# Issuing a mixture's output weights from ScalarE's DMA queue

## What is computed

```python
def moe(h, router_w, router_b, w1, w3, w2):
    ...                       # the router gives every token two of 16 experts: comb
    y = jnp.zeros_like(h)
    for e in range(N_EXPERTS):
        y = y + comb[:, e:e + 1] * ((jax.nn.silu(h @ w1[e]) * (h @ w3[e])) @ w2[e])
    return y
```

## Time and profile before

| | us |
|---|---|
| median of three runs | 1736.25 |
| lowest, highest | 1732.82, 1738.97 |
| the profiled execution, its own time | 1744.38 |
| its span in the trace | 1742.8 |
| PE busy | 1582.3 (91%) |
| ACT busy | 342.9 (20%) |
| SyncE's queue (q1): bytes, share of the 16 DMA engines | 322.90 MB, 52.0% |
| ScalarE's queue (q10) | 10.31 MB, 1.7% |

### The profile page before, as it was taken

One profiled execution on the slowest core, in us unless ns is written; L12 is line 12 of the kernel. 1 busy time (PEld: TensorE's weight loads), 2 busy tenths in 40 slices (PEclk: granted clock), 3 DMA queues, 4 the chain that ended last, 5 costly groups with the idle time before them and its releaser, 6 DMA issues.

```text
span 1742.8 us, 27293 instructions
## 1 busy us (share of the span) xinstructions
PE 1582.3 (91%) x11510; PEld 1119.3 (64%) x11510; DVE 592.6 (34%) x1457; ACT 342.9 (20%) x760; POOL 81.6 (5%) x131
## 2 busy tenths in 40 slices
PE   6999999999889999999796799999849998899987
PEld 5787678876634856745443699998736575455544
DVE  2514422334245247105715111111055543233223
ACT  1313211122131123025204000000042223000000
POOL 0010000100110000000100200000010001000000
PEclk9899898999989899988898899999959998899999
DMA  8366353656765321120730699999783113999996
GB/s 257 94 202 194 124 158 92 197 169 207 199 193 167 101 95 50 49 73 1 229 135 29 256 386 401 394 402 392 314 292 118 73 49 108 338 391 388 391 402 270
DMA packets 180762, 365.11 MB, mean 210 GB/s; under 512 B 18868, under 2 KB 137488, under 8 KB 164160
## 3 DMA queue, kind: packets, MB, share of 16 engines
q1 hardware_dynamic: 164640, 322.90, 52.0%
q0 software_dynamic: 9984, 30.63, 5.5%
q10 hardware_dynamic: 6048, 10.31, 1.7%
HBM read 343.42 MB, written 20.40 MB: 209 GB/s over the span
## 4 chain that ended last, share of the span: by engine, by line
PE 77%; DMA 8%; DVE 8%; ACT 3%; issue 2%; POOL 1%; SPq 0%; POOLq 0%; ACTq 0%; DVEq 0%
PE ps_proj L622 30%; PE ps_outp L622 13%; PE ps_proj L1192 7%; PE ps_outp L1192 7%; PE ps_score L1192 7%; DMA ring<-in_exp_w 4%; PE ps_score L622 2%; PE ps_turn L775 2%; PE ps_outp L1294 2%; PE ps_proj L748 2%; DMA h_t<-in_exp_w 1%; PE ps_score L793 1%; DVE probs L2085 1%; DMA arena<-expert_in 1%; DMA ring<-in_w_in 1%
## 5 line engine op out<-in xcount | busy, mean ns | idle before, releaser
L622 PE MATMUL ps_proj<-h_t,ring 128*128 128x256 f32 (+1 forms) x1280 | 363.1, 444 | 13.6 <-ACT h_t L1733 8.1
L622 PEld LDWEIGHTS ps_proj<-h_t,ring 128*128 128x128 f32 x1280 | 252.3, 199 | 119.9 <-issue 84.9
L1192 PE MATMUL ps_proj<-ring,arena 128*32 128x128 f32 (+2 forms) x1824 | 127.3, 390 | 4.7 <-ACT arena L1882 2.5
L1192 PE MATMUL ps_outp<-ring,arena 128*32 128x384 f32 (+3 forms) x1600 | 123.4, 415 | 3.9 <-DVE arena L2455 3.2
L1192 PE MATMUL ps_score<-ring,arena 128*32 128x384 f32 (+2 forms) x1824 | 123.1, 381 | 4.1 <-DMA ring<-in_exp_w 4.1
L1192 PEld LDWEIGHTS ps_proj<-ring,arena 128*32 128x32 f32 (+1 forms) x1824 | 110.1, 117 | 22.2 <-issue 12.7
L1192 PEld LDWEIGHTS ps_score<-ring,arena 128*32 128x32 f32 (+1 forms) x1824 | 102.9, 114 | 24.5 <-issue 13.3
L1192 PEld LDWEIGHTS ps_outp<-ring,arena 128*32 128x32 f32 (+1 forms) x1600 | 88.3, 115 | 31.1 <-DVE arena L2455 5.6
L622 PE MATMUL ps_proj<-ring,h_t 128*128 128x256 f32 (+1 forms) x512 | 107.6, 368 | 0.4 <-ACT arena L1759 0.4
L622 PEld LDWEIGHTS ps_proj<-ring,h_t 128*128 128x128 f32 x512 | 93.9, 195 | 14.9 <-issue 3.6
L1579 ACT ACTIVATE arena<-ps_proj 128x512 f32<-128x512 f32 (+1 forms) x68 | 39.0, 576 | 324.1 <-PE ps_proj L622 323.2
(11 more groups left out here) (327 smaller groups left out, 1764.6 us busy)
## 6 DMA issues: line engine op xcount, KB each, us to landing
ring<-in_exp_w SPq DMA_DIRECT2D x152, 1024.0 KB, 11.3
ring<-in_ada_w SPq DMA_DIRECT2D x48, 1024.0 KB, 5.4
ring<-in_w_in SPq DMA_DIRECT2D x30, 1024.0 KB, 6.1
arena<-in_exp_w SPq DMA_DIRECT2D x30, 1024.0 KB, 18.4
ring<-in_even_w_in SPq DMA_DIRECT2D x12, 1024.0 KB, 6.6
h_t<-in_exp_w SPq DMA_DIRECT2D x10, 1024.0 KB, 19.9
ring<-in_w_out SPq DMA_DIRECT2D x8, 1024.0 KB, 5.6
expert_in<-arena POOLq DMA_DIRECT2D x1, 6144.0 KB, 31.0
```

The costliest lines, as they stand in the source:

```text
L622: last = pe.matmul(out, w, a, start=(i == 0), stop=(i == len(pairs) - 1))
L1192: last = pe.matmul(b[p0:p0 + pn, c0:c0 + wn], x_of(p0, lo, pn), w[:, w0:w0 + wn], start=first and p0 not in strip[:i], stop=done and p0 no ...
```

## The change

The output blocks from number 10 on (out 1 to out 15, 30 of the 96) are no longer issued by SyncE. ScalarE issues both halves of out e in its own program, right behind the silu of gate e. The wait for the place stays the same, but it stands on ScalarE now, behind the silu. `block_load` returns at once for these blocks. The blocks of out 0 (6 and 7) stay with SyncE, and places, sizes, semaphores and PE's program stay as they were.

```diff
@@ -1889,6 +1889,14 @@
                         if e:
                             act.wait_ge(drained["score"], mark["up", e - 1])
                         act.activation(silu_t[:, 0:256], b[:, 0:256], ACT.Silu).then_inc(drained["proj"], 1)
+                        for half in range(2):
+                            i = INDEX["out", e, half]
+                            if i >= PLACES:
+                                dst, done, _ = blocks[i]
+                                act.wait_ge(*slot_end["last", i - PLACES])
+                                act.dma_start(dst.rearrange("p (k n) -> p k n", k=2),
+                                              dr["exp_w2_2"][l][e].rearrange("(k p) n -> p k n", p=P)[:, 2 * half:2 * half + 2, :]
+                                              ).then_inc(done, 16)
                     if e:
                         b = filled_bank("turn", mark["pick", e - 1])
                         act.activation(pick_t, b[:, 0:S], ACT.Copy).then_inc(drained["turn"], 1)
@@ -2891,6 +2899,8 @@
 
                 kind, e, half = BLOCKS[i]
                 dst, done, _ = blocks[i]
+                if kind == "out" and i >= PLACES:
+                    return
                 if i >= PLACES:
                     sp.wait_ge(*slot_end["last", i - PLACES])
                 elif i >= EXTRA:
```

## The result

| | before | changed |
|---|---|---|
| median, us | 1735.72 (4 runs) | 1759.02 (4 runs) |
| lowest, highest | 1732.82, 1738.97 | 1749.30, 1760.88 |
| ratio, 95% interval | | 1.011 (1.0074 to 1.0146) |
| span of the profiled execution | 1742.8 | 1759.1 |

The kernel is slower, by 1.1% in this comparison. In a later comparison with 12 runs of the changed kernel and 35 of the one before the medians were 1751.70 and 1739.56, ratio 1.0065 (1.0041 to 1.0089). The two intervals overlap between 1.0074 and 1.0089, so the loss is near 0.8%. The kernel before spread from 1726 to 1754 us over all comparisons, so four runs on a side are few.

A forecast was written before the change was run, and what follows sets the result against it. PE and the saturated weight stream were taken to bind the second mixture nearly equally. Terms +5.6 (start), +2.5 (order and end) and -1.0 (rows of expert 1) gave +7.1 on 1736.25, 1743.3 us; range 1735.5 to 1749.5.

The forecast's parts named there:

- What bounds the kernel: Second mixture: PE and the weight stream bind nearly equally; the stream never runs dry, at 2.81 us a block.
- The start: Before gate 1's end: out 1 issued 14 us later, 84 blocks to come in place of 82, costing 5.6 us.
- The order: Each expert: out e gets half the stream and lands some 14 us after gate e, in time; PE waits at gate.
- The end: Gate 15's second half lands at 1724.2, PE waits 8.1 us longer; order and end together add +2.5.
- What it gives back: Before gate 1: expert 1's rows land earlier, taken at 1 us; faster gate 1, up to 2.2, not counted.
- Costs taken at nothing: ScalarE's two issues, its moved place wait, SyncE's relief and GpSimd's sharing with two queues: each counted as 0.
- The sum: Whole kernel: +5.6 (start), +2.5 (order and end), -1.0 (rows of expert 1), +7.1 us, giving 1743.3.
- rival 5: Two queues of weights cost bandwidth, 1.5% or 3.5 us more: +10.6, 1747; chance 0.08.
- rival 1: Order does no harm, blocks come in order of need; up 15's second half is tightest: +3.8, 1740; chance 0.13.
- rival 2: Stream has slack outside the profile, PE sets the end: 0 to +2, 1737; chance 0.12.
- rival 4: Start gain of 5.8 meets a stream with slack, so the kernel is faster: -5.8, 1730.5; chance 0.05.
- rival 3: Expert 1's rows earliest (3.6) and gate 1 at full clock (2.2): +2.3, 1738.5; chance 0.07.

The follow-up runs named there:

- experiment 2: Kernel before, with SyncE issuing out e in its old place but only when gate e is done: 1745.39 us, ratio 1.0015 to before.
- experiment 4: Changed kernel, but out 1 (blocks 12 and 13) stays with SyncE: 1752.91 us, ratio 1.0078 to before.
- experiment 13: Changed kernel, but gate 2 (blocks 10 and 11) is issued only when gate 1 is done: 1760.60 us, ratio 1.0102 to before.
- experiment 1: Changed kernel with output weights read in 8 KB pieces instead of 4 KB, result wrong: 1739.63 us, ratio 0.9999 to before.
- experiment 6: Changed kernel with the second mixture's gate and up weights in 4 KB pieces instead of 8 KB, result wrong: 1735.41 us, ratio 0.9996 to before.
- the second trace: Trace from running the changed kernel again without any edit: median 1751.70 us, ratio 1.0065 to before.
- experiment 11: Kernel before, but SyncE issues blocks 10 to 13 only when expert 1's rows have landed: 1735.07 us, ratio 0.9980 to before.
- experiment 7: Kernel before with the second mixture's output weights read in 8 KB pieces, result wrong: 1739.48 us, ratio 1.0007 to before.
- experiment 12: Kernel before, run once more without an edit for a second trace: 1738.84 us.

## Why the prediction was wrong

**What bounds the kernel** was right: DMA share 1.01 and 392 GB/s again, with no gap from 1514 to 1724 us. By how much a block that is issued late at the start moves the end is less certain: experiments 2, 4 and 13 all moved it the way that the stream's length says, and none by the amount.

**The start** was right in kind. The engines run empty before gate 1's end (0.44 over 17 us), ScalarE issues out 1 at 1499.15, right behind gate 1, and from there 84 blocks are to come. The stream's pace was 2.83 us a block (78 blocks from gate 1's end at 1499.12, which is 1493.45 plus 5.67, to 1720.0); counted the same way, the kernel before has 2.84 (82 blocks from 1495.7 to 1728.5), and the 2.81 of the sum leaves out the first landing. The size of the term is not confirmed. Experiment 2 pays for the same two blocks with 2.7 us, not 5.6. The sum took the pace as fixed, and it is not: from 8 us after silu of gate 1 to 20 us before silu of gate 15 the DMA engines moved 390 GB/s in both traces of before, 395 in experiment 2, 394 and 393 in the changed kernel, 398 and 395 in experiments 1 and 6. A rate 1.3% higher is 2.9 us of 222. Why it differs stays open.

**The order** is the step that failed, in the sentence "at half the rate the two blocks of out e take 4 x 2.81 = 11.2 us ... they land some 14 us after gate e, in time". They get little more than a third, 0.37 of the bytes while both queues have blocks waiting. Two blocks at a third are 6 x 2.83 = 17 us, plus some 2 to 3 until the first data and with GpSimd's rows between: 18.5 to 21.5 measured up to out 13, and 8.4 to 9.4 from the first block to the second, three block times. I had looked at how long the transfers of other queues take and taken that they take turns as taking equal bytes. They take turns by packets, nearly one for one, and the size of a packet stands in the address pattern of each load: one run of 8 KB against two of 4 KB. The page of the kernel before had a hint of it, since it counts packets and bytes for each queue. The Trainium skill's page "DMA: Bandwidth & Descriptors", section "Queues, rings and completion order", says that an engine goes round the queues at packet granularity. I cited it as agreeing and did not ask how large the packets are. The nearly equal packet counts of the short window (261 and 257) agree with it, and experiments 1 and 6 from both sides.

**The end** followed from that step. The forecast had PE's last wait at gate 15's second half, with 92 blocks landed and 26.7 us to go. It was at out 13's second half (1720.06), with 90 landed (gate 15's second half at 1719.6, out 13's at 1720.0; out 14, up 15 and out 15 missing) and 39.0 us to go, 37.4 without the slow end. Before, it was 88 landed and 34.0 to go. From the end of gate 1 to the last wait 78 blocks took 220.9 us, where 74 blocks had taken 213.1: +7.8. With 37.4 less 34.0, +3.4, this is the +11.2 that stands where the sum had +8.1. Out 14 had not jumped ahead of gate 15, as the forecast had it: it was issued at 1715.7 and landed 11 to 13 us later. Put plainly: SyncE's gate and up blocks now land early, at 9 to 10 us in the median (12.6 for those in h_t), and fill the places, while the output block that PE needs next is always the last of the six. A stock of the wrong blocks shortens nothing.

**Luck.** Experiments 1 and 6 have the shares on which the sum was built. From gate 1 to the end they took 253.4 and 254.1 us where before took 247.0; less the slower matmuls of out 15 (6.19 and 5.38 us for 3.70) that is +3.8 and +5.4, where the sum had +8.1. The timed ratios are 0.9999 and 0.9996, where +7.1 us is 1.0041, outside both intervals. So the sum was too high for its own picture and left out the loss that came. The two errors have opposite signs, and by them the forecast lies nearer to the result than its reasoning does.

**What it gives back** was taken at 1.0 and is 2.4: in the second trace 1.4 come from the rows of expert 1 (6.71 for 8.12 us), 0.6 from gate 1 (5.38 for 6.01) and the rest from the transposes before it. The range of 0 to 5.8 for it held; experiment 11 shows 7.7 for the larger edit.

**Costs taken at nothing**: ScalarE's issues took 0.42 to 0.58 us and up to 0.9, and no wait of PE moved to what stands behind them. Right. The waits for places never held.

**The sum** for the mixture comes to 11.8 - 2.4 = +9.4 from the two traces with equal scatters, at an equal end, where the forecast was +7.1. The timed ratio of 1.0065 is +11 us, that of the first four runs +19 to +23. The forecast's 1743.3 stood on a median of 1736.25, the first comparison's changed kernel on four runs of which three were above 1757, where twelve later ones had their median at 1751.7. So the range missed for two causes that are to be kept apart: the order's term, too small by 3 to 4 us (11.2 or 11.8 for 8.1), and the spread of the runs. The table shows parts that differ between two runs of one kernel: how early the mixture begins (1462 to 1475 us with nothing changed ahead of it), a scatter of 3.8 or 10 us, and the clock at the end. A range of +-7 us was too narrow for a median of four runs of this kernel. Against rival 5, the changed kernel's mixed queues moved 392 GB/s as one queue had, so bandwidth was not lost; rival 1 fell with the waits at out, rivals 2 and 4 with the 17.6 us of waits, and of rival 3's gain of 5.8 came 2.4.

## What to carry to other kernels

Before a load is moved to another queue, lay its contiguous run (the packet) beside those of the queue it will meet: in a saturated stream its share of the bytes follows its share of the packet sizes (0.37 here where 4 KB met 8 KB, 0.45 and 0.46 where they were equal). Then ask which block is the last of a period, and count the work behind it. A late issue and a thin share may each be free and be dear together, since both eat the same slack. And before a median of a few runs is trusted to half a per cent, look at two traces of the same kernel and see which parts repeat.

## What the runs showed of the hardware

- While both had blocks waiting, two queues with pieces of 8 and 4 KB took nearly equal numbers of packets (261 and 257 in one window), and the one with the smaller ones got 0.37 of the bytes; with equal pieces, of 8 KB or of 4 KB, it got 0.46 and 0.45. The second of two 1 MB blocks then came 4.8 to 8.1 us behind the first, 6.0 and 6.4 in the median, in place of 8.4 to 9.4.
- PE, reading the moving operand 16 bytes apart, took 3.83 us for 16 matmuls of 128x64 by 128x256 that take 1.95 with columns side by side, at a granted clock of 1.00 both times. The Trainium skill's page "SBUF — State Buffer", section "Door 1: The DMA port swizzle", says that each access that crosses to a new 16-byte line pays a penalty; the measured factor here is 1.96.
- GpSimd's scattered rows landed some 3.8 us after the last of their four transfers was issued, in fourteen of seventeen traces, and after 9.8 to 10.2 in three (the changed kernel's first, experiments 7 and 12). It divides by one thing: in these three SyncE had issued gate 2 some 0.6 us before that last transfer (1477.58 against 1478.18 in the changed kernel), in the others 2.7 us or more after it (1478.60 against 1475.91 before). Which of the two comes first depends on how fast gate 0 runs: 3.67 us in the three, 5.49 us or more in the others but one. That one is experiment 13: gate 0 in 3.67 us, gate 2 held back, and the scatter in 3.77. It is one trace, and in the changed kernel; the kernel before with this alone was not tried.
